# Input rows at one place within 256 bytes for four blocks, and weight chunks shifted in their slots

## The reference

```python
# first block
z = rms_norm(h, norm_mix_w) @ w_in                # 2048 x 11264, split into gates and heads
y_a = hgrn2 (8 heads of 128), norm, gate
y_b = banded attention (16 heads of 64) with relative bias
merged = gate_a * (y_a @ w_branch_a) + gate_b * (y_b @ w_branch_b)
h = h + merged @ w_out
h = h + square(relu(rms_norm(h, norm_mlp_w) @ w_up)) @ w_down     # width 8192
h = rms_norm(h, norm_final_w)
# second block: 16 meta tokens ahead of the 256
proj = rmsnorm(h, pre_norm_g) @ w_in_2            # 2048 x 6656
ya = GQA attention, 8 heads of 128 on 2 key heads, rotary
yb = differential attention, 8 heads: softmax(s1) - lam * softmax(s2), head norm
h = h + rmsnorm([ya, yb] @ w_out_2, post_norm_g)
return h[:, 16:]
```

## Time and profile before

| | us |
|---|---|
| median of 3 runs | 1969.51 |
| lowest, highest | 1966.8, 1970.71 |
| the profiled execution, its time | 1974.29 |
| its span, first to last instruction | 1972.5 |
| TensorE busy with matmuls | 1935.5 |
| DVE busy | 1122.5 |
| ACT busy | 896.2 |

### The profile page before, as it was taken

How to read it: one execution, slowest core, us unless ns; L and a number is a source line. 1 busy time by engine, 2 the same in 40 slices (tenths; PEclk the granted TensorE clock), 3 DMA queues, 4 the chain that set the end, 5 groups by cost and what they waited for, 6 DMA issues and landing times.

```text
span 1972.5 us, 34127 instructions
## 1 busy us (share of the span) xinstructions
PE 1935.5 (98%) x13560; PEld 1786.4 (91%) x13560; DVE 1122.5 (57%) x1219; ACT 896.2 (45%) x1154; POOL 188.7 (10%) x111
## 2 busy tenths in 40 slices
PE   8999999999999999999999999999999999989998
PEld 8989998898899988988998899899889998889986
DVE  6557877366645655455445444545565447656654
ACT  6433333366544445443443344344554345645543
POOL 1002443200000100100010000000000000021100
PEclk9999999999999999999999999999999999989999
DMA  8665555565465666656665565566565654334554
GB/s 265 184 178 159 164 168 157 160 179 149 140 214 181 206 202 185 195 193 192 193 192 192 172 187 187 188 186 194 191 187 169 178 161 129 107 104 121 162 187 144
DMA packets 175990, 345.36 MB, mean 175 GB/s; under 512 B 10816, under 2 KB 11024, under 8 KB 175328
## 3 DMA queue, kind: packets, MB, share of 16 engines
q1 hardware_dynamic: 174160, 337.76, 55.3%
q0 software_dynamic: 1696, 5.64, 1.0%
HBM read 341.26 MB, written 2.10 MB: 174 GB/s over the span
## 4 chain that ended last, share of the span: by engine, by line
PE 94%; DVE 3%; ACT 2%; issue 1%; DMA 0%; POOLq 0%; SPq 0%; POOL 0%; DVEq 0%; ACTq 0%
PE ps L396 56%; PE ps L408 31%; PE ps L480 1%; DVE wlo L1156 1%; PE ps L709 1%; ACT whi L802 1%; PE ps L537 0%; PE ps L673 0%; PE ps L696 0%; PE ps L527 0%; PE ps L426 0%; PE ps L519 0%; PE ps L518 0%; DMA x_nat<-in_x_dram 0%; PE ps L684 0%
## 5 line engine op out<-in xcount | busy, mean ns | idle before, releaser
L1156 DVE TENSOR_TENSOR wlo<-raw,whi 128x1024 fp32r<-128x1024 f32 x632 | 818.3, 1301 | 745.5 <-ACT whi L802 744.8
L802 ACT ACTIVATE whi<-raw 128x1024 fp32r<-128x1024 f32 x632 | 665.4, 1058 | 938.9 <-PE ps L396 599.5
L396 PE MATMUL ps<-xhi,whi 128*128 128x256 f32 (+1 forms) x1984 | 572.3, 288 | 0.0
L396 PE MATMUL ps<-xhi,wlo 128*128 128x256 f32 (+1 forms) x1984 | 560.6, 283 | 0.0
L396 PE MATMUL ps<-xlo,whi 128*128 128x256 f32 (+1 forms) x1984 | 560.5, 283 | 0.0
L396 PEld LDWEIGHTS ps<-xhi,whi 128*128 128x128 f32 x1984 | 376.9, 190 | 12.7 <-issue 11.7
L396 PEld LDWEIGHTS ps<-xlo,whi 128*128 128x128 f32 x1984 | 376.6, 190 | 1.4 <-issue 0.5
L396 PEld LDWEIGHTS ps<-xhi,wlo 128*128 128x128 f32 x1984 | 376.2, 190 | 0.0
L396 PE MATMUL ps<-x2lo,whi 128*128 128x256 f32 x1024 | 284.6, 278 | 2.3 <-issue 2.3
L396 PE MATMUL ps<-x2hi,whi 128*128 128x256 f32 x1024 | 284.7, 278 | 0.6 <-issue 0.6
L396 PE MATMUL ps<-x2hi,wlo 128*128 128x256 f32 x1024 | 284.6, 278 | 0.0
(11 more groups left out here) (335 smaller groups left out, 2239.9 us busy)
## 6 DMA issues: line engine op xcount, KB each, us to landing
raw<-in_w_in_dram SPq DMA_DIRECT2D x280, 512.0 KB, 3.8
raw<-in_w_up_dram SPq DMA_DIRECT2D x128, 512.0 KB, 3.7
raw<-in_w_down_dram SPq DMA_DIRECT2D x128, 512.0 KB, 4.0
raw<-in_w_out_dram SPq DMA_DIRECT2D x64, 512.0 KB, 4.1
raw<-in_w_branch_a_dram SPq DMA_DIRECT2D x16, 512.0 KB, 5.1
raw<-in_w_branch_b_dram SPq DMA_DIRECT2D x16, 512.0 KB, 4.0
x_nat<-in_x_dram SPq DMA_DIRECT2D x4, 512.0 KB, 7.1
rel<-in_rel_bias_dram POOLq DMA_DIRECT2D x8, 256.0 KB, 4.2
```

The costliest lines, as they stand in the source:

```text
L396: ins = mm(outs[b], w[:, k % SLOTS, j, cols], v[:, kt, 0:n], start=start, stop=last and j == CK - 1 and i == 2, skip_group_check=True)
L802: f(whi[:, k % SLOTS], raw[:, k % SLOTS], ACT.Copy).then_inc(whi_ready, 1)
L1156: tt(wlo[:, k % SLOTS], raw[:, k % SLOTS], whi[:, k % SLOTS], ALU.subtract).then_inc(wlo_ready, 1)
```

## The change

Input block kt moves to row `x_row(kt)` = 4 (kt mod 4) + kt div 4 of xhi and xlo. Rows 4 apart lie 4,352 bytes, 17 times 256, apart, so the blocks 0 to 3 share one place within 256 bytes, 4 to 7 the next, 64 bytes on, and so forth. The chunk with blocks kt = 2k and 2k + 1 is written and read in its slot with a shift of 16 elements (64 bytes) times k div 2, in the first and the second projection only (`w_shift`). `whi` grows by 256 bytes and `wlo` by 192; 64 bytes (`arena_place`) fill up, so that the buffers behind keep their place within 256 bytes, while xhi and xlo move by 448 bytes.

A shifted chunk reaches into the next slot. Where that slot still holds a chunk with a smaller shift, `w_free` makes ACT's split wait for that chunk too, c - 3 instead of c - 4. That is so for chunks 4, 5 and 6 of each group with shifts.

```diff
+SLOT = CK * CW
+CLASSES = 4
+STEP = TM - T
+REACH = (CLASSES - 1) * STEP
+
+def x_row(kt):
+    return KT // CLASSES * (kt % CLASSES) + kt // CLASSES
+
+def w_shift(c0, k):
+    if isinstance(c0, int) and (c0 + k < C_BR or C_IN2 <= c0 + k < C_OUT2):
+        return STEP * ((c0 + k) % NC // (NC // CLASSES))
+    return 0
+
+def w_slot(ring, c0, k):
+    lo = SLOT * (k % SLOTS) + w_shift(c0, k)
+    return ring[:, lo:lo + SLOT].rearrange("p (j c) -> p j c", j=CK)
+
+def w_free(c0, k):
+    need = c0 + k - SLOTS + 1
+    if isinstance(c0, int) and k % SLOTS < SLOTS - 1 and w_shift(c0, k) > w_shift(c0, k - SLOTS + 1):
+        return need + 1
+    return need
...
-        whi = sb("whi", [P, SLOTS, CK, CW], F32R)
-        wlo = sb("wlo", [P, SLOTS, CK, CW], F32R)
+        whi = sb("whi", [P, SLOTS * SLOT + REACH + STEP], F32R)
+        wlo = sb("wlo", [P, SLOTS * SLOT + REACH], F32R)
         xhi = sb("xhi", [P, KT, TM], F32R)
         xlo = sb("xlo", [P, KT, TM], F32R)
+        sb("arena_place", [P, ARENA_PLACE])
...
-                            ins = mm(outs[b], w[:, k % SLOTS, j, cols], v[:, kt, 0:n], start=start,
+                            ins = mm(outs[b], w_slot(w, c0, k)[:, j, cols], v(kt, slice(0, n)), start=start,
...
-                    act.wait_ge(pe_done, c0 + k - SLOTS + 1)
-                f(whi[:, k % SLOTS], raw[:, k % SLOTS], ACT.Copy).then_inc(whi_ready, 1)
+                    act.wait_ge(pe_done, w_free(c0, k))
+                f(w_slot(whi, c0, k), raw[:, k % SLOTS], ACT.Copy).then_inc(whi_ready, 1)
```

More of the change, by code:

```diff
@@ L37 @@
 SLOTS = 4
+ARENA_PLACE = 16
 LEAD = 4
@@ L413, in chunk_n, with x_high, x_low, rows_of @@
                 return ins
+            def x_high(kt, cols):
+                return xhi[:, x_row(kt), cols]
+            def x_low(kt, cols):
+                return xlo[:, x_row(kt), cols]
+            def rows_of(v):
+                return lambda kt, cols: v[:, kt, cols]
             def blocks(s):
@@ L611, in quarter @@
                             pe.wait_ge(x_ready, KT + CK * (k + 1))
-                        chunk_t(c0 + NC * g, k, CK * k, x2hi, x2lo, blocks(g % 2), T, k == 0, k == NC - 1)
+                        chunk_t(c0 + NC * g, k, CK * k, rows_of(x2hi), rows_of(x2lo), blocks(g % 2), T, k == 0, k == NC - 1)
                 for g in range(4):
@@ L761, in _ @@
                             ins.then_inc(r_mm, 1)
-                    chunk_t(c0, k, CK * k, xhi, xlo, outs, TM if kv else T, k == 0, k == NC - 1, shared=not kv)
+                    chunk_t(c0, k, CK * k, x_high, x_low, outs, TM if kv else T, k == 0, k == NC - 1, shared=not kv)
                     if j == 5 and 1 <= k <= 5:
@@ L811, in row_root, with turned_upper @@
                 f(ss[:, col:col + 2], ss[:, col:col + 2], ACT.Sqrt, bias=eps_t[:], scale=1.0 / D).then_inc(n_sd, 1)
-            def turned_upper(b, n, dst, w):
+            def turned_upper(b, n, dst, w, row):
                 for i in range(4):
@@ L817, in turned_upper @@
                     act.wait_ge(n_tr, KT // 2 * b + kt // 2 + 1)
-                    f(dst[:, kt, 0:T], turned(n, i), ACT.Copy, scale=w[:, kt:kt + 1]).then_inc(n_hi, 1)
+                    f(dst[:, row(kt), 0:T], turned(n, i), ACT.Copy, scale=w[:, kt:kt + 1]).then_inc(n_hi, 1)
             def start_upper(kt):
                 act.wait_ge(n_tr, kt // 2 + 1)
-                f(xhi[:, kt, 0:T], ps[:, 4 + (kt % 8) // 2, (kt % 2) * T:(kt % 2) * T + T], ACT.Copy,
+                f(xhi[:, x_row(kt), 0:T], ps[:, 4 + (kt % 8) // 2, (kt % 2) * T:(kt % 2) * T + T], ACT.Copy,
                   scale=mix_w[:, kt:kt + 1]).then_inc(n_hi, 1)
@@ L928, in _ @@
                         act.wait_ge(m_w, 1)
-                        f(xhi[:, :, T:TM], meta_t[:], ACT.Copy).then_inc(m_hi, 1)
+                        f(xhi_g[:, :, :, T:TM], meta_t[:].rearrange("p (n i) m -> p n i m", n=CLASSES), ACT.Copy).then_inc(m_hi, 1)
                     if g == G_HGOUT and 2 <= k <= 5:
@@ L953, in _ @@
                 act.wait_ge(br_m, n + 1)
-                f(xhi[:, bass.ds(4 * n, 4), 0:T], both[:], ACT.Copy).then_inc(br_hi, 1)
+                f(xhi_g[:, bass.ds(n, 1), :, 0:T], both[:].rearrange("p (o i) t -> p o i t", o=1), ACT.Copy).then_inc(br_hi, 1)
             def h_squares(n, free, done, into):
@@ L975, in _ @@
                     if n >= 1 and k == 1:
-                        turned_upper(1, n - 1, x2hi, mlp_w)
+                        turned_upper(1, n - 1, x2hi, mlp_w, same_row)
             def quarter(q, first=False, last=False):
@@ L987, in quarter @@
                             if k == 1:
-                                turned_upper(1, 3, x2hi, mlp_w)
+                                turned_upper(1, 3, x2hi, mlp_w, same_row)
                             if k == 5:
@@ L1155, in split_lo, with turned_lower @@
                 dve.wait_ge(whi_ready, c0 + k + 1)
-                tt(wlo[:, k % SLOTS], raw[:, k % SLOTS], whi[:, k % SLOTS], ALU.subtract).then_inc(wlo_ready, 1)
-            def turned_lower(b, n, dst, hi, w):
+                tt(w_slot(wlo, c0, k), raw[:, k % SLOTS], w_slot(whi, c0, k), ALU.subtract).then_inc(wlo_ready, 1)
+            def turned_lower(b, n, dst, hi, w, row):
                 for i in range(4):
@@ L1162, in turned_lower @@
                     dve.wait_ge(n_hi, KT * b + kt // 2 * 2 + 2)
-                    stt(out=dst[:, kt, 0:T], in0=turned(n, i), scalar=w[:, kt:kt + 1], in1=hi[:, kt, 0:T],
+                    stt(out=dst[:, row(kt), 0:T], in0=turned(n, i), scalar=w[:, kt:kt + 1], in1=hi[:, row(kt), 0:T],
                         op0=ALU.mult, op1=ALU.subtract).then_inc(x_ready, 1)
@@ L1168, in start_lower @@
                 dve.wait_ge(n_hi, kt // 2 * 2 + 2)
-                stt(out=xlo[:, kt, 0:T], in0=ps[:, 4 + (kt % 8) // 2, (kt % 2) * T:(kt % 2) * T + T],
-                    scalar=mix_w[:, kt:kt + 1], in1=xhi[:, kt, 0:T], op0=ALU.mult,
+                stt(out=xlo[:, x_row(kt), 0:T], in0=ps[:, 4 + (kt % 8) // 2, (kt % 2) * T:(kt % 2) * T + T],
+                    scalar=mix_w[:, kt:kt + 1], in1=xhi[:, x_row(kt), 0:T], op0=ALU.mult,
                     op1=ALU.subtract).then_inc(x_ready, 1)
@@ L1387, in _ @@
                 dve.wait_ge(br_hi, n + 1)
-                tt(xlo[:, bass.ds(4 * n, 4), 0:T], both[:], xhi[:, bass.ds(4 * n, 4), 0:T],
+                tt(xlo_g[:, bass.ds(n, 1), :, 0:T], both[:].rearrange("p (o i) t -> p o i t", o=1), xhi_g[:, bass.ds(n, 1), :, 0:T],
                    ALU.subtract).then_inc(br_ready, 1)
@@ L1396, in _ @@
                     if n >= 1 and k == 1:
-                        turned_lower(1, n - 1, x2lo, x2hi, mlp_w)
+                        turned_lower(1, n - 1, x2lo, x2hi, mlp_w, same_row)
                 dve.wait_ge(pe_done, c0 + NC)
@@ L1409, in quarter @@
                             if k == 1:
-                                turned_lower(1, 3, x2lo, x2hi, mlp_w)
+                                turned_lower(1, 3, x2lo, x2hi, mlp_w, same_row)
                             if k == 4:
```

28 lines of the change are left out of this document (16 added, 12 removed).

## The result

| | before | after |
|---|---|---|
| median, us | 1970.11 | 2055.2 |
| ratio, with its 95% interval | | 1.0439 [1.0423, 1.0455] |
| the profiled execution, us | 1974.29 | 2052.67 |
| its span, us | 1972.5 | 2050.7 |
| mean granted clock | 0.994 | 0.984 |

The median of before is that of the runs made beside the changed kernel. A few executions ran far outside the rest (3878.1 us, one of the four of before; 8362.05, one of the four of after; 1 of 12 with wide slots, 2 of 7 in the last experiment), and they count in the medians given here but not in the ratios.

What follows compares the result with a forecast made beforehand. TensorE was taken as the bound: the number of matmuls times the spacing of their starts. 1974.3 - 18 + 72 + 2 + 31 = 2061, or 2056.5 against the median of 1969.5; forecast range 2040 to 2078, chance 0.58.

Steps and rivals of the forecast that it cites:

- less cover: Both projections: faster TensorE chunks cover less of the side work in the tight stretch; +2 to +3, taken as 2 us.
- Term 1: Both projections: x at 192 bytes from the weights everywhere brings matmul starts closer; -18 us, bounds 0 to -26.
- three quarters of 22.0: 256-column form: 4,992 matmuls could gain 22.0 us; one slow x2 quarter seen, so three quarters taken, 16.5.
- rival 2: Projections: the spacing does not come, as x's place alone or the loop's locked phase may count; 2072 us, chance 0.14.
- Term 2: ACT's splits of chunks 4, 5, 6 wait one more TensorE chunk, delaying queued attention work; +72 us, bounds 58 to 85.
- first kind: Second attention's units with scores next: scores start 4.0 us late at positions 1 to 3 and 9 to 11; 24 us.
- second kind: Second attention, positions 33 to 35 and 41 to 43: late copy out stops TensorE 2.9 us each; 17.5 us.
- banded attention: First attention: ACT's late copy delays L537 by 1.76 us, the minimum adds up to 0.4; five groups, 10.5 us.
- uncertain places: Head norm of the first kind, turn of the values, row scales: five places, 0 to 4.0 us each, half taken, 10.
- early groups: Decay levels and early groups have more than two chunks of cover; 0 to 5 us, taken as 3.
- Term 3: Slow clock after added TensorE stops: 16 stops at 1.9 us each; +31 us, bounds 0 and 48.
- Rivals 1, 3 and 4: 1: clock stays up, 2025 us, 0.14; 3: wait hidden, 1951, 0.05; 4: more slow stretches than counted, 2086, 0.09.

Runs made afterwards that it cites:

- wide slots: The changed kernel with slots 256 bytes further apart and without the added wait; 1970.14 us, ratio to before 1.0009.
- the waits alone: The kernel before with only the added waits at chunks 4, 5 and 6 of each group, no address changed; 2054.33 us, ratio 1.045.
- rows alone: The changed kernel's order of input rows, without the weight shift and without the added wait; 1976.16 us, ratio to before 1.0028.
- the second execution: The kernel before, unchanged, run and traced once more; 1964.97 us.
- the other way: The last experiment: wide slots with its four places in the opposite order, so each change goes 64 bytes down; 1961.56 us, ratio to before 0.9955.

## Why the prediction was right, and where its sizes were off

The forecast, 2056.5, is 1.3 us from the median, and the mechanism is the one it named: the whole loss is reproduced by the waits alone. That it came so near is luck. All three terms are off: the first by 14 us in one direction, the other two by 12 and 10 in the other. Of the 8 us that this leaves, 6.7 are hidden by the choice of executions that were profiled, 78.4 us apart (1974.29 and 2052.67) where the medians are 85.1 apart. Against the profiled execution of before:

| term | predicted | measured |
|---|---|---|
| 1, spacing | -18 | -4 |
| 2, added wait, with its 2 us of less cover | +74 | +62 |
| 3, granted clock | +31 | +21 at most |
| sum | +87 | +79 |

**Term 1.** It was the step "three quarters of 22.0" that failed. From x2's quarters I took it that at 192 bytes a quarter of the matmuls would be slow. But x2 never changes its place and x changes it every 48 matmuls, and each undisturbed change ends the fast spacing (24 of 24 in after and with wide slots). The 256-column form gained 3,380 x 0.86 + 1,390 x 2.35 = 6.2 us, not 16.5. The 272-column form gained 2.1 us, where I took 1.5; the swapped form 1.1. Then come stages that I had at nothing: the branches, the first quarter up and down and the second output lost 3.4 + 3.4 + 1.7 + 1.5 = 10.0, while the third quarter of before, slow in its profiled run, was fast in after, 3.4 + 1.7 = 5.1 back. -9.4 + 10.0 - 5.1 = -4.5. Beside an execution of before in which the third quarter is fast, the change gains nothing, which is what the kernel with wide slots shows over many runs.

So rival 2, "the spacing does not come", was nearer to the truth of the whole kernel than the forecast's term. Of its two reasons, that the place of x alone counts falls: four rows of x at one place, the same in both kernels, never ran under 119.4 ns with the weights unshifted (the part at 0 bytes in the run with rows alone) and ran at 113.6 in a group with wide slots, where the weights are shifted with them. The other, the phase in which the loop happens to lock, is what the runs show, and it acts beside the distance. The independent ports of which the Trainium skill speaks (TensorE: Matmul & The Clock Gate, "Step-by-step: what each phase is for") would, as the prediction read them, make the distance nothing; with rows alone moved, one and the same shape runs at 114.0 ns at 192 bytes and 119.6 at 0, so that reading does not hold here. No run shows by what path the distance acts.

**Term 2.** Position by position, from the matched starts of before and after:

| | predicted | measured |
|---|---|---|
| first kind, positions 1 to 3 | 3 x 4.0 | 3.92, 3.68, 3.50 |
| first kind, 9 to 11 | 3 x 4.0 | 3 x 2.92, and 0.84 once |
| positions 17 to 19 | 7 | 2.92, 3.80 |
| second kind, 6 positions | 6 x 2.9 | 5 x 2.92, 2.70, then 1.2 given back |
| banded attention, a position | 1.76 | 1.66 in four, and 3.4 of smaller ones (10.1 for the predicted 10.5) |
| uncertain places | 10 | 8, and 1.2 given back |
| early groups | 3 | 2 |

The second kind came out to 0.02 us; the rule "its start moves to the next split's start, and everything in the queue with it" is exact where the copy out is last. In the first kind it was one step too far: at positions 9 to 11 TensorE stops for 2.92 us at the values, ahead of the scores, and then spends time on values and turns in which the minimum catches up; the scores stopped for themselves only once, for 0.84. I had noted that the values stop first and still charged the scores' 4.0 for all three. The 2 us for less cover fell away with term 1.

**Term 3.** The price was right and the count was not. 42.6 us more at the lower level cost at most half of that, 21 us, for 11 more spells: 1.9 us each, the figure taken. I had 16 spells, one for each stop of some 3 us; but of the six stops of the second kind only one was followed by a spell (two of the six in the run with the waits alone), though all are of 2.7 to 2.9 us. The row from which I took the price could have warned me, had there been a second trace: before's stop of 2.58 us that ends at 1724.73 was followed by a spell in the profiled execution, and the same stop in the second execution was not. In the windows above the clock stayed full through 1858 to 1873.

**Rivals 1, 3 and 4.** The clock did not stay up (0.984 against 0.994, 42.6 us more at the lower level). The wait was not hidden: the stops came where ACT's queue was read to be the path, and with the waits alone. More slow stretches than counted did not come; there were fewer.

**The signs to look for.** ACT's splits 8 to 9 us apart: 9.0 and 9.1. TensorE's waits for the minimum, the copy out and ACT's pt in the second attention, 50 to 60 us: 43.9 in the rows above, and 52.2 with the 8.3 at L763, which I had not named; too high by the six scores. Mean clock near 0.98: 0.984. Groups near 21.7 us: 22.10, the one sign that failed, and the one on which term 1 stood. One reading of the earlier trace rows was too narrow: the same list also has 6.8 us of DMA and 3.0 of issue, all outside the second attention. Nothing in the sum rests on it.

## What to carry to other kernels

A wait on an in-order queue is not paid by its own instruction but by what is queued behind it: compare the end of the queued work, moved to the new start, with the moment at which the next engine wants it. A layout that needs such a wait must first be tried with the wait taken out by room, here 256 bytes a slot; that showed in one experiment that the layout was worth nothing yet, and a change of its order then gave 0.45%. And a spacing read from one execution may be a state rather than a price: look at the same stage in several executions before a term is built on it.

## What the runs showed of the hardware

- Where the input's rows lie 192 bytes past the weights within 256, long rows of these matmuls run at one of two spacings and keep it: 113.3 or 117.8 ns at 256 columns, 228.9 or 233.3 at 512, 4.4 ns apart in both, at the full clock and with the same instructions and addresses. In the kernel with wide slots one row of 1,030 matmuls ran at 117.8 throughout. Within one place no chunk change altered it in the kernels with wide slots and the other way (114 of 114); in after 1 of 55 did.
- The fast spacing of the 256-column form was seen only at those 192 bytes. At the other seven multiples of 32 the means were 116.8 to 119.8 ns. 192 itself does not force it. Only the 256-column form was measured at the other distances one by one.
- A change of place of both operands by 64 bytes ended the fast spacing 65 of 65 times in wide slots and the other way. The slow one it ended 26 of 26 times downwards, in one kernel, and 8 of 43 upwards (35 of 166 over the four kernels that go up).
- What sets the state at the start of a row was not settled. A matmul more ahead of it, or an unshifted group ahead of the branches, turned it over, each seen in one trace; for the most part the program repeats it (16 of 16 groups alike in two traces); that the third quarter differs between two executions of one kernel says that the program alone does not fix it. Why down and up differ is open too; nothing here was tried that looks at it.
- Stops of equal length, 2.7 to 2.9 us, are followed by a spell at the lower clock in some places and not in others, and one stop of 2.58 us in one execution of before and not in the other. No run here tells why.
